# A decoder block with 256 expert gathers: the last modulation chunk in four dead pieces, the second tile's attention spread over 24 gather slots, norm rows by TensorE

## The reference

```
mod = silu(c) @ w_ada + b_ada            # 6 x 1024: sh1 sc1 g1 sh2 sc2 g2
h = x * (1 + sc1) + sh1
q, k, v (two head groups) = h @ w_in
y = [rms(attention group 0), rms(attention group 1)] @ w_out
x1 = layer_norm(alpha * x + (1 + g1) * y) * ln1_g + ln1_b
h2 = x1 * (1 + sc2) + sh2
# PEER: per token and head (8), top 16 of 128 x 128 product keys -> 128 experts per token
e, g = top-k of (h2 @ w_q) against sub_keys
f = sum over the 128 (head, k):  gelu(h2 . u[e]) * g * v[e]
out = layer_norm(alpha * x1 + (1 + g2) * f) * ln2_g + ln2_b
```

## Time and profile before

| | |
|---|---|
| median of three runs | 847.32 us (843.36 to 852.72) |
| the profiled execution | 853.17 us, of it 851.3 us span |
| first gather issued | 163.61 us |
| last dot | 838.40 us |
| PE, DVE, ACT, POOL busy | 84%, 67%, 40%, 33% |
| moved by DMA | 327.95 MB, of it 268.45 MB gathers |
| mean granted TensorE clock | 0.969 |

### The profile page before, as it was taken

The page is one execution under the profiler, slowest core; times in us unless marked ns, Lnnn a source line. Parts: engine busy times, 40 slices in busy tenths (PEclk is TensorE's granted clock), DMA queues, the critical chain, the costliest instruction groups (busy, mean ns, idle before and its releaser), DMA issues.

```text
span 851.3 us, 7305 instructions
## 1 busy us (share of the span) xinstructions
PE 716.4 (84%) x2042; PEld 341.3 (40%) x2042; DVE 567.1 (67%) x1289; ACT 343.9 (40%) x998; POOL 281.1 (33%) x260
## 2 busy tenths in 40 slices
PE   5999999689999888898987777878878877878784
PEld 2866855445445344444432222322223222222221
DVE  6675646858858667867675768767666757675454
ACT  0032031247655434434443435443435444343333
POOL 0000000114334544544354434444343444334420
PEclk9999999779999999999999999899999999999998
DMA  9999964469999999999999999999999999999991
GB/s 355 403 422 422 390 258 158 159 262 356 386 387 416 421 423 421 421 421 420 422 421 420 422 422 421 420 423 421 421 421 421 423 420 421 423 421 421 421 421 80
DMA packets 47895, 327.95 MB, mean 385 GB/s; under 512 B 5552, under 2 KB 7920, under 8 KB 8688
## 3 DMA queue, kind: packets, MB, share of 16 engines
q0 software_dynamic: 36864, 268.45, 76.5%
q1 hardware_dynamic: 10256, 58.73, 17.2%
q10 hardware_dynamic: 736, 0.32, 0.1%
HBM read 326.40 MB, written 1.07 MB: 385 GB/s over the span
## 4 chain that ended last, share of the span: by engine, by line
DMA 45%; PE 36%; DVE 8%; ACT 6%; issue 3%; SPq 1%; ACTq 0%; POOL 0%; DVEq 0%; POOLq 0%
DMA ring<-in_experts,e_all 42%; PE bank L441 19%; PE bank L433 8%; DMA ring<-in_w 3%; DVE ring L759 3%; PE bank L464 3%; DVE acc L854 3%; ACT diag L611 2%; PE bank L538 1%; PE bank L519 1%; ACT weight L607 1%; PE bank L509 1%; PE bank L526 1%; SPq L348 1%; ACT gel L603 1%
## 5 line engine op out<-in xcount | busy, mean ns | idle before, releaser
L441 PE MATMUL bank<-ring,diag 128*128 128x512 f32 x1024 | 501.3, 624 | 99.3 <-ACT diag L611 99.1
L971 POOL DMA_INDIRECT ring<-in_experts,e_all x256 | 280.9, 1097 | 542.8 <-PE bank L441 354.7
L441 PEld LDWEIGHTS bank<-ring,diag 128*128 128x128 f32 x1024 | 183.3, 194 | 394.1 <-ACT diag L611 232.2
L759 DVE CUSTOM_DVE_ANT_0 ring<-ring,T_h 128x1024 f32<-128x1024 f32 x128 | 156.7, 1225 | 112.9 <-DMA ring<-in_experts,e_all 112.9
L759 DVE CUSTOM_DVE_ANT_0 ring<-ring,h 128x1024 f32<-128x1024 f32 x128 | 156.6, 1223 | 95.7 <-DMA ring<-in_experts,e_all 95.6
L603 ACT ACTIVATE gel<-pre 128x1 f32<-128x1 f32 x256 | 51.9, 203 | 331.1 <-DVE pre L759 330.3
L611 ACT ACTIVATE diag<-consts,weight 128x128 f32<-128x128 f32 x256 | 102.7, 401 | 8.4
L607 ACT ACTIVATE weight<-gel,g_all 128x1 f32<-128x1 f32 x256 | 75.4, 295 | 9.3
L854 DVE SCALAR_TENSOR_TENSOR acc<-ring,cact,acc 128x512 f32<-128x512 f32 x77 | 57.9, 752 | 3.5
L433 PE MATMUL bank<-ring,hT_yT 128*128 128x512 f32 x80 | 38.9, 640 | 3.5 <-DMA ring<-in_w 1.8
L464 PE MATMUL bank<-hT_yT,lnw 128*128 128x256 f32 x128 | 30.6, 401 | 1.1 <-DVE hT_yT L838 1.1
(11 more groups left out here) (146 smaller groups left out, 532.4 us busy)
## 6 DMA issues: line engine op xcount, KB each, us to landing
ring<-in_w SPq DMA_DIRECT2D x32, 1024.0 KB, 14.0
lnw<-in_w SPq DMA_DIRECT2D x6, 1024.0 KB, 16.4
ring<-in_experts,e_all POOLq DMA_INDIRECT x256, 15.0
H_s<-in_w SPq DMA_DIRECT2D x3, 1024.0 KB, 25.3
mod<-in_w SPq DMA_DIRECT2D x2, 1024.0 KB, 26.6
H_s<-scratch SPq DMA_DIRECT2D x1, 2048.0 KB, 26.6
mod<-in_b_ada_r SPq DMA_DIRECT2D x1, 2048.0 KB, 23.3
lnw<-in_ln SPq DMA_DIRECT2D x1, 2048.0 KB, 11.2
```

The lines of the kernel that those rows point to most:

```text
L441: last = nc.tensor.matmul(tile_sum(t)[n], diag[:, i % DIAGS, :], ring[:, RING_AT[i], D + CH * n:D + CH * n + CH], start=(s == 0), stop=(s ...
L759: nc.vector.tensor_tensor_reduce(ring[:, r, 0:D], ring[:, r, 0:D], h2[i // SLOTS], 1.0, 0.0, ALU.mult, ALU.add, pre[:, i % PAIR:i % PAIR + ...
L971: nc.gpsimd.indirect_dma_start(ring[:, r, :], None, A["experts"], bass.IndirectOffsetOnAxis(ap=e_all[:, i:i + 1], axis=0)).then_inc(slot_i ...
```

## The change

- The last chunk of `w_ada`, `("ada", 11)`, has no ring place any more. It is loaded in four pieces of 0.5 MB into memory that nothing uses at that time (h2 of tile 0, y of tile 1, a quarter of the Hankel table, V of tile 1), right behind `ln1` in SP's queue, and so ahead of `("out", 1)` and `("q", 0)`.
- `("wsum", 10)` goes ahead of `("S", 2)`, and `("wsum", 11)` to just behind `("v", 1, 0)`. `free 0` now stands behind `("v", 1, 1)` and waits for no sum.
- Unit 4's `S` goes ahead of `("q", 0, 0)`, its `Tr` ahead of `("modrow", 7)`, its `PV` ahead of the slots. `("q", 0, 1)` and its scores go in between the pieces of head 0, behind the one with the exponential.
- The units 5 to 11 stand at slots 0 to 23 instead of 0 to 19; the projection of tile 1 at 27 to 33 instead of 22 to 28, `("q", 0, 2)` at 35 instead of 32. `free 4` moves from slot 29 to 36, and `WIDE_FROM` from 36 to 42: six places serve the gathers 0 to 41.
- `xa`, `ln1a`, `ln1b` and `x1` are cut into halves at slots of their own, with a wait between the gated product and its use.
- The norm rows are loaded onto one partition (16 KB), and eight steps `lnb` (a PE product with ones of 128x512, a copy on ACT) spread them, four from slot 44 and four from slot 112.
- Tile 1's queries and key scores go at slots 72 to 107; both tiles use one place for the scores, and ACT waits for the picks of tile 0 before it writes over them.

```diff
-WIDE_FROM = 36
+WIDE_FROM = 42
...
-       ("v", 1, 0), ("modrow", 5), ("madd", 5), ("wsum", 10), ("Tr", 2), ("Tr", 3), ("wo", 0, 0, 0), ("PV", 2), ("PV", 3), ("ny", 0),
-       ("wo", 0, 0, 1), ("yT", 0, 1), ("modrow", 6), ("xa", 0), ("wo", 0, 1, 0), ("wo", 0, 1, 1), ("rows2",), ("madd", 6), ("ln1a", 0),
-       ("v", 1, 1), ("ln1b", 0), ("hT", 0, 0), ("hT", 0, 1), ("wsum", 11), ("q", 0, 0),
-       ("s", 0, 0, 0), ("s", 0, 0, 1), ("modrow", 7), ("free", 0), ("q", 0, 1), ("s", 0, 1, 0), ("s", 0, 1, 1)]
-    + [("piece", 0, j) for j in range(PIECES)]
-    + [("free", 1), ("madd", 7), ("S", 4), ("S", 5), ("v", 0, 1), ("free", 2)]
+       ("wsum", 9), ("qk", 3, 0), ("modrow", 3), ("madd", 3), ("modrow", 4), ("madd", 4), ("qk", 3, 1), ("wsum", 10), ("S", 2), ("S", 3),
+       ("v", 1, 0), ("wsum", 11), ("modrow", 5), ("madd", 5), ("Tr", 2), ("Tr", 3), ("wo", 0, 0, 0), ("PV", 2), ("PV", 3), ("ny", 0),
+       ("wo", 0, 0, 1), ("yT", 0, 1), ("modrow", 6), ("xa", 0, 0), ("xa", 0, 1), ("wo", 0, 1, 0), ("wo", 0, 1, 1), ("rows2",), ("madd", 6), ("ln1a", 0, 0), ("ln1a", 0, 1),
+       ("v", 1, 1), ("free", 0), ("ln1b", 0, 0), ("ln1b", 0, 1), ("hT", 0, 0), ("hT", 0, 1), ("S", 4), ("q", 0, 0),
+       ("s", 0, 0, 0), ("s", 0, 0, 1), ("Tr", 4), ("modrow", 7)]
+    + [("piece", 0, j) for j in range(EXP_PIECE + 1)]
+    + [("q", 0, 1), ("free", 1), ("s", 0, 1, 0), ("s", 0, 1, 1)]
+    + [("piece", 0, j) for j in range(EXP_PIECE + 1, PIECES)]
+    + [("madd", 7), ("S", 5), ("PV", 4), ("v", 0, 1), ("free", 2)]
...
 BESIDE = {
-    0: [("Tr", 4)], 1: [("Tr", 5)], 2: [("PV", 4), ("PV", 5)],
-    3: [("S", 6), ("S", 7)], 5: [("Tr", 6), ("Tr", 7)], 7: [("PV", 6), ("PV", 7)], 9: [("S", 8), ("S", 9), ("yT", 1, 1)],
-    11: [("Tr", 8), ("Tr", 9)], 13: [("PV", 8), ("PV", 9)],
-    15: [("S", 10), ("S", 11)], 17: [("Tr", 10), ("Tr", 11)], 19: [("PV", 10), ("PV", 11)], 20: [("ny", 1)], 21: [("yT", 1, 0)],
-    22: [("wo", 1, 1, 1)], 24: [("wo", 1, 1, 0)], 25: [("xa", 1)], 26: [("wo", 1, 0, 1)], 28: [("wo", 1, 0, 0)], 29: [("free", 4), ("ln1a", 1)],
-    31: [("ln1b", 1)], 32: [("q", 0, 2)], 34: [("s", 0, 2, 0)], 35: [("s", 0, 2, 1)], 37: [("hT", 1, 0)], 38: [("hT", 1, 1)],
+    0: [("Tr", 5)], 2: [("PV", 5)],
+    5: [("S", 6), ("S", 7)], 7: [("Tr", 6), ("Tr", 7)], 9: [("PV", 6), ("PV", 7)], 11: [("yT", 1, 1)],
+    12: [("S", 8), ("S", 9)], 14: [("Tr", 8), ("Tr", 9)], 16: [("PV", 8), ("PV", 9)],
+    19: [("S", 10), ("S", 11)], 21: [("Tr", 10), ("Tr", 11)], 23: [("PV", 10), ("PV", 11)], 24: [("ny", 1)], 25: [("yT", 1, 0)],
+    27: [("wo", 1, 1, 0)], 29: [("wo", 1, 1, 1)], 30: [("xa", 1, 0)], 31: [("wo", 1, 0, 0)], 32: [("xa", 1, 1)], 33: [("wo", 1, 0, 1)],
+    34: [("ln1a", 1, 0)], 35: [("q", 0, 2)], 36: [("free", 4), ("ln1a", 1, 1)], 37: [("s", 0, 2, 0)], 38: [("ln1b", 1, 0), ("s", 0, 2, 1)],
...
             sp.dma_start(ln1.rearrange("p r c -> p (r c)"), A["ln"][:, 0:2 * D].broadcast_to([P, 2 * D])).then_inc(ln1_in, 16)
+            sp.wait_ge(hT_ready, KC)
+            last = A["w"][CHUNK[("ada", 11)]].rearrange("p (k n) -> p k n", k=KC)
+            for i, patch in enumerate(patches):
+                sp.dma_start(patch, last[:, 2 * i:2 * i + 2]).then_inc(patch_in[i], 16)
             filled(sp, ("qk", 3, 1))
             load(("out", 1))
             summed(sp, 10)
             load(("q", 0))
-            filled(sp, ("v", 1, 1))
-            load(("ada", 11))
...
-            sp.dma_start(lnw[:].rearrange("p r c -> p (r c)"), A["ln"].broadcast_to([P, 4 * D])).then_inc(lnw_in, 16)
+            sp.dma_start(lnw[0:1].rearrange("p r c -> p (r c)"), A["ln"]).then_inc(lnw_in, 16)
...
+                elif kind == "lnb":
+                    r, n = step[1:]
+                    pe.wait_ge(lnw_in, 16)
+                    nc.tensor.matmul(dst[:], ones[0:1, :], lnw[0:1, r, CH * n:CH * n + CH], start=True, stop=True).then_inc(full, 1)
```

More of the change, by code:

```diff
@@ L216, in build @@
         ln1 = H_s[:, NT * D:].rearrange("p (r c) -> p r c", r=2)
+        patches = [tile.rearrange("p (k n) -> p k n", n=CH) for tile in (h2_0[:], xT_y[:, D:2 * D], H_s[:, 0:D], V_x1[:, 1, :])]
         halves = {"high": (T_h2[:, NT * D:], H_s[:, NT * D:])}
@@ L273, in build @@
         lnw_in = sem("lnw_in")
+        patch_in = [sem(f"patch_in{i}") for i in range(len(patches))]
         wq_in = {"high": sem("wq_high_in"), "low": sem("wq_low_in")}
@@ L668, in _ @@
                                          scale=1.0 / CH).then_inc(sq_ready, 1)
-                elif kind == "ln1a":
+                elif kind == "lnb":
+                    r, n = step[1:]
+                    evacuate(step, lnw[:, r, CH * n:CH * n + CH], filled(act, step)[:])
+                elif kind == "ln1a" and step[2] == 1:
                     t = step[1]
@@ L765, in route @@
                 t, h = divmod(head, PH)
-                both = scores[:, t, h]
+                both = scores[:, h]
                 cube = [P, 2, TOPK, TOPK]
@@ L848, in _ @@
                     part = acc[:, c % 4, :]
-                    own.then(nc.vector.tensor_scalar(part, w[:, 0, :], cact[:, 0:1], None, ALU.mult))
+                    first = patches[0][:, 0, :] if patched else w[:, 0, :]
+                    own.then(nc.vector.tensor_scalar(part, first, cact[:, 0:1], None, ALU.mult))
                     for k in range(1, KC):
-                        if k == KC // 2:
+                        if patched and k % 2 == 0:
+                            dve.wait_ge(patch_in[k // 2], 16)
+                        if not patched and k == KC // 2:
                             arrived(dve, n, 1)
                         own.settle()
-                        ins = nc.vector.scalar_tensor_tensor(part, w[:, k, :], cact[:, k:k + 1], part, ALU.mult, ALU.add)
+                        row = patches[k // 2][:, k % 2, :] if patched else w[:, k, :]
+                        ins = nc.vector.scalar_tensor_tensor(part, row, cact[:, k:k + 1], part, ALU.mult, ALU.add)
                         if k < KC - 1:
@@ L894, in _ @@
                 elif kind == "xa":
-                    t = step[1]
-                    dve.wait_ge(x_in, 16)
-                    dve.wait_ge(sq_ready, t + 1)
-                    own.then(nc.vector.reciprocal(ystat[:, t, 2, :], ystat[:, t, 1, :]))
-                    own.settle()
-                    gate(t, FIRST[t])
-                    for n in range(2):
-                        settle_bank(dve, ("wo", t, FIRST[t], n))
-                        half = slice(CH * n, CH * n + CH)
-                        own.then(nc.vector.scalar_tensor_tensor(x[:, t, half], x[:, t, half], ALPHA, acc[:, n, :], ALU.mult, ALU.add))
+                    t, n = step[1:]
+                    if n == 0:
+                        dve.wait_ge(x_in, 16)
+                        dve.wait_ge(sq_ready, t + 1)
+                        own.then(nc.vector.reciprocal(ystat[:, t, 2, :], ystat[:, t, 1, :]))
+                    half = gate(t, FIRST[t], n)
+                    own.then(nc.vector.scalar_tensor_tensor(x[:, t, half], x[:, t, half], ALPHA, acc[:, n, :], ALU.mult, ALU.add))
                 elif kind == "rows2":
@@ L953, in _ @@
                     t = step[1]
+                    for r in range(2, 4):
+                        for n in range(2):
+                            settle_bank(dve, ("lnb", r, n))
                     centre(NT + t, V_x1[:, t, :], lnw[:, 2, :], h2[t])
```

71 lines of the change are left out of this document (41 added, 30 removed), and 6 rows, old and new, of the table BESIDE.

## The result

| | before | changed |
|---|---|---|
| median | 849.31 us (20 runs, 843.36 to 853.34) | 843.60 us (20 runs, 841.42 to 846.59) |
| ratio | | 0.9929, 95% interval 0.9913 to 0.9944 |
| profiled execution, its span | 853.17, 851.3 us | 843.37, 841.6 us |

The change makes the kernel 0.7% faster, 5.7 us between the medians. The forecast was 1.5% and 835 us, reckoned from a median before of 847.32 us (three runs); with 20 runs that median is 849.31. The two profiled executions lie 9.8 us apart, 4 us more than the medians do. Where that comes from is half of this study.

The account below looks back on a forecast made before the run. DMA engines bind at 421 GB/s, 2.49 us a gather, after 15.3 us of early starving. Gains 2.1 + 7 + 1.5 + 5.0 less 3 make 12.6 us: 840.6 from 853.17, 835 on the median's scale; range 825 to 850.

Parts of the forecast that it names:

- 0.985 of before, and 835 us on the scale of the median: Whole kernel: 840.6 us on the profiled execution's scale of 853.17, carried over to the median of 847.32; chance 0.50.
- The norm rows, 5.0 us less to carry: Norm-row load: 2048 KB become 16, so 2.1 MB at 421 GB/s is saved, 5.0 us; the replacing steps cost nothing.
- the rows' bytes were hidden anyway: Rival, block from 257 us: TensorE set the pace there, so the 5 us count only in part; 844 us, chance 0.13.
- Six places for 42 gathers, 3 us of loss: Slots 27 to 36: TensorE 10.8 us over, stock and query weights cover most; 3 us of loss (0 to 7).
- First gather 161.3, gain 2.1: Start of gathers: VectorE's wait for wsum 11's chunk goes, first gather 161.3 instead of 163.61; gain 2.1 us (0 to 3.5).
- The first slots, 7 us: Gathers 4 to 9: earlier v(0,1) and slot 0 cut starving from 10.6 to 3.6 us; gain 7 us (2.6 to 9).
- the units over 24 slots, 1.5: 200 to 240 us: less unit work per slot cuts starving from 4.7 to 3.2 us; gain 1.5 us (0 to 3).
- The pause behind v(0,1): TensorE's gap ahead of the product that ran at 179.22 us: stays of the same size, 2.66 us.
- The clock's rival (841): Rival, first slots: TensorE at 1.2 GHz, starving 8 us in place of 3.6; gain 6.7 us, 841 us, chance 0.22.
- The slower rival: Rival, projection block with six places: stock empty at slot 27, all 10.8 us starved; 855 us, chance 0.08.
- VectorE's idle time before the first piece below 1 us: Sign that the forecast is right: VectorE hardly waits ahead of the first piece, below 1 us.
- The sign of dot 37 (274 to 278 us): Sign that the forecast is right: dot of gather 37 at 274 to 278 us instead of 288.65.

Follow-up runs that it names:

- second look: Second profiled execution of an unaltered kernel: of before, 849.15 us, last dot 834.4 us; beside the 6.0 us starved, of the changed kernel, 844.46 us median.
- experiment 6: Kernel before with only the norm rows loaded on one partition and spread by TensorE: 848.46 us, ratio 0.9973 to before.
- experiment 2: Changed kernel with the norm rows loaded spread by DMA as before and no `lnb` steps: 844.71 us, ratio 0.9955 to before.
- experiments 3 and 11: Changed kernel, eight places from gather 36, first-half projections first: 0.9896; projections in own order: 0.9891; old slots, eight from 30: 0.9879; projection block taken apart: 0.9850.
- third look: Third profiled execution of the kernel before, unaltered: 849.32 us, last dot 834.6 us.
- twelve looks: The twelve profiled executions that have the changed first part as it is: gather 0 issued at mean 162.2 us, against 162.7 in the four with the old one.
- experiment 12: No edit; traces compared, twelve with changed first part against four with old: gather 0 to gather 6 took 16.2 to 18.0 us against 22.1 to 22.7.
- experiments 7 and 11: Changed kernel with old slots for tile 1's work: 0.9928; also rows by DMA: 0.9933; old slots, first-half projections first, eight places from gather 30: 0.9879.
- old slots, eight places from 32: Changed kernel with tile 1's work on old slots, first-half projections first, free 4 at slot 25, eight places from gather 32: 848.76 us, ratio 0.9986.

## Why the prediction was wrong

The sum was 12.6 us; the same pair of profiles shows 9.75, the medians 5.7. Two steps failed: what was won against one slow execution was scaled to the median (4.0 us), and the rows' bytes were counted while the block starved without them (from dot 24 on 3.0 us lost where 2.0 were to be won). Up to dot 24 the pair brought 12.8 us where the sum had 10.6.

- **"0.985 of before, and 835 us on the scale of the median": the step that failed first.** I took the whole of one execution's starving as typical and scaled it. 4.0 us of it, the difference of the last dots of before (838.4 against 834.4), arose in the stretch with TensorE's half clock of 180 to 194 us, of which the other two looks had 3.4 us each. That the execution lay 5.9 us above the median then known (3.9 above that of 20 runs) was the hint, and the granted clock of 0.66 was its place; I had put the clock down as a danger of the changed kernel and not as a one-off loss of the profile that I subtracted from. The starving of before between 160 and 240 us is 10.2 us in the second look, not 15.3 (180 x 20 + 109 x 20 + 20 x 40 KB, less 5.4 us ahead of the first byte), and 12.2 us in the third, whose first gather went out 1.7 us earlier. One pair shows the 4.0 us; experiment 6 leaves room for less.
- **"The norm rows, 5.0 us less to carry": fell.** They were worth 0.25 us by experiment 2. The rival "the rows' bytes were hidden anyway", given 0.13 and 844 us, is what happened, and it had the reason right: they passed in the block where TensorE sets the pace. That 843.6 was measured is partly luck: its 844 was 3.3 us under a median of 847.32, and the gain was 5.7.
- **"Six places for 42 gathers, 3 us of loss": too small.** 6.0 us starved, 7.1 in the second look. The mechanism was right, as experiments 3 and 11 show. In its size I had let the query weights' 2.5 us cover; they are issued at 235.1 us and landed by 244.8, while the first projection starts at 242.3, so they pass almost wholly ahead of the block. The two steps can't be added one by one: without rows to carry the starving grows. Together they were to bring 2 us; from gather 24 to the end the lead fell by 3.0 us (12.76 to 9.75).
- **"First gather 161.3, gain 2.1": 0.5 on average.** It went out at 161.6 in one execution of the changed kernel and at 163.08 in the other, where half clock followed the pauses behind S 2. S 2 and w_out's second chunk came at the times worked out. But the kernel before had it at 161.69 in its third look, so 161.3 was no gain of 2.1 against a typical execution. TensorE's product that was to be 1.4 us late starts at 120.5 to 121.8 in the twelve looks, at 117.7 to 119.5 in the four of before; and the scores are 3.1 us later where the sum had 1.5 (experiment 12). And the 1.5 us between two executions were gone at dot 38.
- **The first slots, 7 us, and the units over 24 slots, 1.5: right against this profile, too much against a typical one.** Gather 6 went out at 180.0 (forecast 177.5 to 179), starving up to 200 us was 3.2 us (3.6), and after 200 us 2.2 (3.2). From dot 0 to dot 24 the lead grew by 12.3 us. Against the second look it is 8.1 at dot 24, and spreading the units shows no share of it (experiments 7 and 11). The pause behind v(0,1) was to stay at 2.66 us; it became 3.15.
- The clock's rival (841) did not come in this look: the low clock fell on v(0,1), from 161.9 to 168.7 us, and the slots ran at 2.4 GHz. The danger is not gone, though. In experiment 2 it was 1.2 GHz from 172.8 to 179.6 us, and in "old slots, eight places from 32" from 173.2 to 186.9, with gather 9 at 191.2. The slower rival did not come, though its mechanism, the block with too few places, is what took the gain behind dot 24. The sign "VectorE's idle time before the first piece below 1 us" was badly chosen: with the sum gone, VectorE has nothing to do but wait there, 4.16 us. The sign of dot 37 (274 to 278 us) was met at 275.54 and yet the median missed: like the sum, it was a time on the scale of one execution, and it stood ahead of the end of the block.

Against the second look of before the account is: 8.1 us at dot 24, 5.0 for bytes, -6.0 starved and 0.9 that the second look itself starved between 240 and 271 us (12 x 31 KB), together 8.0. The last dots say 5.8. The other 2.2 us are not traced.

## What to carry to other kernels

Before a term is read off as starving or waiting time, ask whether the execution that shows it is a typical one: a profile that lies 4 us above the median may hold 4 us that the change can't give, and a second look costs less than an argument. The same holds for a wait that is taken away ahead of one event: compare that event over all executions at hand, here the first gather, before its gain is added up. Where transfers and an engine bind in turn, bytes are worth their time only in stretches in which the transfers bind; taken out of a stretch in which the engine binds, they leave a hole (2.1 MB, 0.25 us here). And a ring that grows should grow at a turn of its rotation: grown from six to eight places at gather 38 or 32, which are no multiples of six, it asked for a place filled only four gathers before.

## What the runs showed of the hardware

- TensorE's granted clock differs between executions of one kernel, by when it comes back: after the same pause of 2.66 us it was 1.2 GHz until 194.2 us once, until 184.5 and 183.0 in two others. The pair with the same first gather is 4.0 us apart at the last dot. Over 107 runs of that kernel, those with a mean granted clock of 0.970 or less took 852.0 us on average, those with 0.977 or more 847.7.
- The same pauses can be followed by either clock. After pauses of 1.61 and 0.91 us TensorE ran at 1.2 GHz in the changed kernel (5.30 us for a product of 3.60), and after 1.63 and 0.91 us at 2.4 GHz with the norm rows by DMA (3.60 us).
- A load of ScalarE's table took 1.28 us, and the instruction behind it started 0.02 us after its end or less (before: load at 176.32, gelu at 177.62).
